# MLP up products of three of four chunks as seven products of half blocks, on one Trainium2 core

## What is computed

```python
def sqrelu_mlp(h, w_up, w_down):          # h 512x1024, w_up 1024x4096, w_down 4096x1024
    return jnp.square(jax.nn.relu(h @ w_up)) @ w_down
...
        x = x + rmsnorm(m, g_mix_post[i])
        h = rmsnorm(x, g_ffn_pre[i])
        x = x + rmsnorm(sqrelu_mlp(h, mlp_w_up[i], mlp_w_down[i]), g_ffn_post[i])
```

## Time and profile before

| | us |
|---|---|
| median of 3 runs | 1156.62 (1155.4 to 1156.87) |
| profiled execution | 1155.48 |
| its span, first to last instruction | 1153.3 |
| TensorE busy | 1130.8 (98%) |
| VectorE, ScalarE, GpSimd busy | 902.0, 676.9, 213.4 |

### The profile page before, as it was taken

The page is one execution under the profiler, slowest core; times in us unless marked ns, Lnnn a source line. Parts: engine busy times, 40 slices in busy tenths (PEclk is TensorE's granted clock), DMA queues, the critical chain, the costliest instruction groups (busy, mean ns, idle before and its releaser), DMA issues. The chain is left out here.

```text
span 1153.3 us, 16246 instructions
## 1 busy us (share of the span) xinstructions
PE 1130.8 (98%) x5598; PEld 951.6 (83%) x5598; DVE 902.0 (78%) x1386; ACT 676.9 (59%) x1168; POOL 213.4 (19%) x205
## 2 busy tenths in 40 slices
PE   8999999999999999999999999999999999999997
PEld 7788888888888888888977888878888888888886
DVE  5899965778479578589789888875797588586698
ACT  6778877565344353445787777765565453443453
POOL 5688860300000000002421111100300000000003
PEclk9999999999999999999999999999999999999999
DMA  5322123321522514313223332232424315215301
GB/s 166 100 70 73 37 76 107 113 74 39 180 73 72 171 50 129 128 37 73 56 55 90 80 86 64 82 83 73 146 74 135 120 37 173 84 37 183 109 19 73
DMA packets 104939, 104.66 MB, mean 91 GB/s; under 512 B 4861, under 2 KB 86781, under 8 KB 104874
## 3 DMA queue, kind: packets, MB, share of 16 engines
q1 hardware_dynamic: 103532, 101.29, 27.4%
q0 software_dynamic: 1264, 2.36, 1.2%
q10 hardware_dynamic: 78, 0.16, 0.1%
HBM read 99.34 MB, written 2.10 MB: 88 GB/s over the span
## 5 line engine op out<-in xcount | busy, mean ns | idle before, releaser
L695 PE MATMUL psum<-hhi,whi 128*128 128x512 f32 x760 | 300.1, 395 | 0.8 <-DVE wlo L1825 0.5
L697 PE MATMUL psum<-hhi,wlo 128*128 128x512 f32 x760 | 296.3, 390 | 0.0
L696 PE MATMUL psum<-hlo,whi 128*128 128x512 f32 x760 | 296.1, 390 | 0.0
L1270 ACT ACTIVATE whi<-mraw 128x1024 fp32r<-128x1024 f32 x176 | 185.5, 1055 | 143.1 <-PE psum L992 113.5
L1836 DVE TENSOR_TENSOR wlo<-mraw,whi 128x1024 fp32r<-128x1024 f32 x176 | 214.4, 1224 | 42.5 <-ACT whi L1270 42.5
L990 PE MATMUL psum<-whi,aop_hi 128*128 128x512 f32 x448 | 174.9, 390 | 0.0
L992 PE MATMUL psum<-whi,aop_lo 128*128 128x512 f32 x448 | 174.4, 389 | 0.0
L991 PE MATMUL psum<-wlo,aop_hi 128*128 128x512 f32 x448 | 174.3, 389 | 0.0
L697 PEld LDWEIGHTS psum<-hhi,wlo 128*128 128x128 f32 x760 | 142.6, 188 | 30.4
L695 PEld LDWEIGHTS psum<-hhi,whi 128*128 128x128 f32 x760 | 142.7, 188 | 29.5 <-issue 1.8
L696 PEld LDWEIGHTS psum<-hlo,whi 128*128 128x128 f32 x760 | 142.8, 188 | 28.0
(11 more groups left out here) (268 smaller groups left out, 2040.0 us busy)
## 6 DMA issues: line engine op xcount, KB each, us to landing
mraw<-in_mlp_w_up SPq DMA_DIRECT2D x64, 512.0 KB, 5.0
mraw<-in_mlp_w_down SPq DMA_DIRECT2D x64, 512.0 KB, 4.6
wraw<-in_conv_pw_w SPq DMA_DIRECT2D x20, 512.0 KB, 4.4
wraw<-in_attn_w_in SPq DMA_DIRECT2D x16, 512.0 KB, 5.0
wraw<-in_attn_w_in SPq DMA_DIRECT2D x16, 256.0 KB, 3.2
wraw<-in_attn_w_o SPq DMA_DIRECT2D x8, 512.0 KB, 4.1
xin<-in_x SPq DMA_DIRECT2D x4, 512.0 KB, 7.0
wraw<-in_conv_pw_w SPq DMA_DIRECT2D x8, 256.0 KB, 6.7
```

The costliest lines, as they stand in the source:

```text
L695: pe.matmul(o, whi[:, u, kb, :], xhi, start=start, stop=False)
L696: pe.matmul(o, whi[:, u, kb, :], xlo, start=False, stop=False)
L697: return pe.matmul(o, wlo[:, u, kb, :], xhi, start=False, stop=stop)
L1270: a.activation(split_unit(whi, e), raw_unit(c, e_), ACT.Copy).then_inc(s["m_hi"], 1)
```

## The change

- **Up stage of chunks 2 to 4** (`up_product`): by the same scheme of seven products, over halves of the inner dimension and of the tokens, and for each of two groups of hidden columns (h). A chunk's up stage has 14 units, each of 2 x 4 x 3 matmuls of 256 columns, in the order P1, P7, P6, P2, P5, P4, P3. Partial sums are copied by ScalarE (`copy_product`), added by VectorE (`c_add2`), and relu and square are both ScalarE's (`take`). Forms and rests of two row blocks are made by one instruction (`s7_of` and so on). The first chunk's up stage stays with eight blocks.
- **h's forms**: `h_whole` makes h in xT's place during the first chunk's up stage (8 instructions of 512 columns), `h_sum` the sums S5, S7, S2, S4, `form_hi_of` and `form_rest` the two parts of the seven forms (full-size instructions of ScalarE and VectorE). As xT is overwritten, x goes to HBM before (`x_copy`) and comes back at the start of the last down stage.
- **Weight sums**: P5 and P6 by VectorE, P7 and P4 by DMAs with addition from HBM, issued by GpSimd (`block_sums`, 28 of 512 KB per MLP), for the down stages too.
- **Numbering**: 106 units per MLP instead of 88; from unit 7 on, unit e goes to buffer (e + 2) % 4, so units 7 and 8 wait for two units more than the others do. Raw slots rotate in another order, and loads are issued by half slots. The first chunk's up columns are loaded in pairs from its two halves.
- A few entries of the attention's hand-written orders move. Some semaphores are used twice.

The diff, cut:

```diff
-UNITS = 22
-MLP_UNITS = CHUNKS * UNITS
+DOWN_UNITS = 14
+UP_OF = (UP_UNITS, 14, 14, 14)
+BASE = (0, 22, 50, 78)
+DOWN = tuple(b + u for b, u in zip(BASE, UP_OF))
+MLP_UNITS = 106
+SHIFT_AT = 7
+def slot(e):
+    return (e if e < SHIFT_AT else e + 2) % 4
...
+UP_ORDER = (P1, P7, P6, P2, P5, P4, P3)
+UP_BLOCK = {P1: B11, P7: B12, P6: B11, P2: B21, P5: B12, P4: B11, P3: B22}
+UP_AT = {i: n for n, i in enumerate(UP_ORDER)}
...
+                for j, b in enumerate((B11, B21, B12, B22)):
+                    for h in range(2):
+                        down_half(0, b, h, 2 * j + 2)
+                    if j == 1:
+                        sp.wait_ge(s["x_done"], (KB, 3 * KB)[l])
+                        sp.dma_start(x_copy, flat(xT[:, :, :])).then_inc(x_kept, 16)
+                for c in range(1, CHUNKS):
+                    n, u = DOWN[c - 1], BASE[c]
+                    for b, at_ in ((B12, 3), (B11, 9), (B21, 11), (B22, 13)):
+                        for h in range(2):
+                            up_half(c, b, h, n + at_ + h)
+                    for h in range(2):
+                        for b, at_ in ((B11, P2), (B21, P5), (B12, P4), (B22, P3)):
+                            down_half(c, b, h, u + 7 * h + UP_AT[at_] + 1)
+                sp.wait_ge(s["m_unit"], MLP_UNITS * l + DOWN[CHUNKS - 1])
+                sp.dma_start(flat(xT[:, :, :]), x_copy).then_inc(x_kept, 16)
...
-            ("T", 7), ("P", 10), ("P", 11), ("O", 1)]
+            ("P", 10), ("T", 7), ("P", 11), ("O", 1)]
...
-ACT_LAST = [("SPLIT", 2), ("S", 0), ("X", -1), ("S", 1), ("T", 0), ("S", 2), ("S", 3), ("T", 1), ("VSPLIT", 0),
+ACT_LAST = [("SPLIT", 2), ("S", 0), ("S", 1), ("X", -1), ("SPLIT", 3), ("T", 0), ("S", 2), ("S", 3), ("T", 1), ("VSPLIT", 0),
...
+            def add_up(l, c, i, h):
+                r = up_slots(l, c)
+                if i == P7:
+                    pool.wait_ge(*loaded(r[B12], h, 2 * (CHUNKS * l + c) + 1))
+                    pool.wait_ge(v7_sum[h], 16 * (v7_nth(l, c, "up", h) - 1))
+                    g.dma_start(raw_half(r[B12], h, 2 * P), up_block(l, c, B22, h),
+                                accum_op=ALU.add).then_inc(v7_sum[h], 16)
+                else:
+                    pool.wait_ge(s["m_ready"], MLP_UNITS * l + BASE[c] + 7 * h + UP_AT[P6] + 1)
+                    pool.wait_ge(s["t_sum"], t_nth(l, c, "up", 2 * h + 1))
+                    g.dma_start(raw_half(r[B11], h, 2 * P), up_block(l, c, B21, h),
+                                accum_op=ALU.add).then_inc(v4_sum[h], 16)
...
+            def block_sums(l):
+                for c in range(CHUNKS):
+                    for i in (P7, P4):
+                        for h in range(2):
+                            add_down(l, c, i, h)
+                        for h in range(2 if c < CHUNKS - 1 else 0):
+                            add_up(l, c + 1, i, h)
...
+            def up_product(l, c, h, i):
+                e, n = BASE[c] + 7 * h + UP_AT[i], 3 * l + c - 1
+                pe.wait_ge(s["m_ready"], MLP_UNITS * l + e + 1)
+                pe.wait_ge(form_lo, lo_nth + 7 * l + H_NTH[FORM[i]])
+                if i == P1:
+                    pe.wait_ge(s["p_evac"], 5 * (CHUNKS * l + c))
+                    bank = Y_BANK[h]
...
+                for t in range(2):
+                    o = by_tile(bank)[:, t, :]
+                    for k in range(4):
+                        w = slice(k * 2 * P + t * P, k * 2 * P + (t + 1) * P)
+                        first = i in (P1, P7) and t == 0 and k == 0
+                        pe.matmul(o, wh[:, w], xh[:, k, :], start=first, stop=False, skip_group_check=True)
+                        pe.matmul(o, wh[:, w], xl[:, k, :], start=False, stop=False, skip_group_check=True)
+                        mm = pe.matmul(o, wl[:, w], xh[:, k, :], start=False, stop=k == 3, skip_group_check=True)
+                mm.then_inc(s["m_unit"], 1)
...
-                    act.wait_ge(s["m_unit"], MLP_UNITS * l + e - 3)
...
+                    act.wait_ge(s["m_unit"], MLP_UNITS * l + e - (1 if e in (SHIFT_AT, SHIFT_AT + 1) else 3))
...
+            def take(l, c, h, q):
+                g, n = CHUNKS * l + c, 3 * l + c - 1
+                at_ = pair[:, 2 * h:2 * h + 2, C_SLOT[q], :]
+                if q in (C11_, C12_):
+                    i, bank = (P2, X_COPY) if q == C11_ else (P3, Y_BANK[h])
+                    act.wait_ge(s["m_unit"], MLP_UNITS * l + BASE[c] + 7 * h + UP_AT[i] + 1)
+                    from_ = by_tile(bank)
+                else:
+                    act.wait_ge(c_sum2, sum2_nth + 4 * n + 2 * h + (1 if q == C22_ else 2))
+                    from_ = at_
+                nth = 8 * n + 4 * h + q + 1
+                a.activation(at_, from_, ACT.Relu,
+                             scale=-1.0 if q in (C12_, C22_) else 1.0).then_inc(c_taken, 1)
+                act.wait_ge(c_taken, taken_nth + nth)
+                a.activation(at_, at_, ACT.Square).then_inc(s["a_sq"], 1)
...
+                n = DOWN[0]
+                for i, forms in enumerate(((A11, S7), (A12,), (S2,), (S5, A22), (S4,))):
+                    m_hi(l, n + 4 + 2 * i)
+                    m_hi(l, n + 5 + 2 * i)
+                    if i < 4:
+                        keep_product(l, i)
+                    for form in forms:
+                        form_hi_of(l, form)
+                m_hi(l, n + 14)
+                keep_product(l, P7)
+                m_hi(l, n + 15)
+                m_hi(l, n + 16)
...
+                for c in range(1, CHUNKS):
+                    g, n = CHUNKS * l + c, BASE[c]
+                    m_hi(l, n + 3)
+                    m_hi(l, n + 4)
+                    copy_product(l, c, 0, CX)
+                    m_hi(l, n + 5)
+                    copy_product(l, c, 0, CZ)
+                    m_hi(l, n + 6)
+                    copy_product(l, c, 0, CU)
+                    m_hi(l, n + 7)
+                    take(l, c, 0, C11_)
+                    m_hi(l, n + 8)
+                    take(l, c, 0, C22_)
+                    m_hi(l, n + 9)
+                    take(l, c, 0, C21_)
+                    m_hi(l, n + 10)
+                    take(l, c, 0, C12_)
+                    a1_hi_of(g, 0)
...
+                    m_hi(l, n + 16)
+                    take(l, c, 1, C21_)
+                    a1_hi_of(g, 1)
+                    take(l, c, 1, C12_)
+                    m_hi(l, n + 17)
+                    a2_hi_of(g, 1)
+                    m_hi(l, n + 18)
+                    s_hi_of(g, 1)
...
+            def add_up_block(l, c, i, h):
+                r, half = up_slots(l, c), slice(h * D, (h + 1) * D)
+                at_ = MLP_UNITS * l + BASE[c] + 7 * h
+                b11, b12 = mraw[:, r[B11], half], mraw[:, r[B12], half]
+                if i == P6:
+                    dve.wait_ge(s["m_ready"], at_ + UP_AT[P1] + 1)
+                    dve.wait_ge(v7_sum[h], 16 * v7_nth(l, c, "up", h))
+                    d.tensor_tensor(b11, b11, b12, ALU.add).then_inc(s["t_sum"], 1)
+                else:
+                    dve.wait_ge(s["m_ready"], at_ + UP_AT[P7] + 1)
+                    dve.wait_ge(s["t_sum"], t_nth(l, c, "up", 2 * h))
+                    dve.wait_ge(*loaded(r[B22], h, 2 * (CHUNKS * l + c) + 1))
+                    d.tensor_tensor(b12, b11, mraw[:, r[B22], half], ALU.subtract).then_inc(s["t_sum"], 1)
+            def h_whole(l, k):
+                if k == 0:
+                    dve.wait_ge(x_kept, 16 * (kept_nth + 2 * l + 1))
+                d.scalar_tensor_tensor(xT[:, k, :], xT[:, k, :], vcol(V_FFN_PRE + l, k), rinv[:, :], ALU.mult,
+                                       ALU.mult).then_inc(h_made, 1)
+            def h_sum(l, form):
+                first = made_nth + 12 * l + KB
+                o = form_of[form]
+                if form == S5:
+                    dve.wait_ge(h_made, first)
+                    d.tensor_tensor(o, form_of[A22], form_of[S7], ALU.subtract).then_inc(h_made, 1)
+                if form == S7:
+                    dve.wait_ge(h_made, first + 1)
+                    d.tensor_tensor(o, form_of[A11], o, ALU.subtract).then_inc(h_made, 1)
...
+            def form_rest(l, form):
+                o = form_of[form]
+                d.tensor_tensor(form_low[form], o, form_high[form].bitcast(F32), ALU.subtract).then_inc(form_lo, 1)
...
+            def first_up(l):
+                g = CHUNKS * l
                 for i in range(4):
                     relu(g, 2 * i)
-                    if early:
-                        if i:
-                            s_lo(g, i - 1)
+                    if i:
+                        s_lo(g, i - 1)
+                    if i < 3:
                         relu(g, 2 * i + 1)
                         m_lo(l, i + 6)
                         s7(g, i)
                     else:
-                        if c == 0:
-                            s_lo(g, i - 1)
-                        m_lo(l, n + 2 * i + 3)
+                        m_lo(l, 9)
```

(81 more changed lines are left out.)

557 lines of the change are left out of this document (370 added, 187 removed).

## The result

The changed kernel takes 1182.12 us (median of four runs, 1181.17 to 1182.78) against 1156.21 us (1155.4 to 1156.87) for the kernel before on the same chip: ratio 1.0223, 95% interval 1.0211 to 1.0236. The forecast was 1165.5 us with a range of 1149 to 1180. The direction was right; the size was not: +26 us where +9 had been worked out, 2 us above the top of the range.

A forecast was written before the change was run, and what follows sets the result against it. TensorE, busy 1130.8 of 1153.3 us, was taken as the bound: 1155.5 - 19.2 (Part 1) + 22.2 (Part 2) + 6 (Part 3), plus 1.1 from trace to median, gave 1165.5 us; range 1149 to 1180.

The forecast's parts named there:

- Part 1: Up stages of chunks 2 to 4: 336 matmuls of 256 columns at 0.120 us replace 192 of 512, saving 19.2 us.
- Rival E: Up stages: halved matmuls take half of a long one, 0.1134 us, saving 32.5 us, total 1152.3 us; chance 0.03.
- Part 2: First chunk of each MLP: buffer step, `h_whole` and `h_sum` delay VectorE's splits, costing 11.1 us per MLP, 22.2 in all.
- the walk: Step-by-step timing of engine queues; first chunk has `m_lo(12)` 10.1 us late, later chunks have a tight up stage end.
- Part 3: End of the new up stages: TensorE waits 1.0 us, mainly for unit 19's split, six times, 6 us; bounds 0 to 15.
- Rival D: TensorE's 4.0 us standstill in the first down stage drops the clock, adding at most 1 us per MLP; within the forecast's 0.68.
- Part 4: Adding transfers land in 5 to 8 us and cost nothing; ScalarE may wait for P4's weights to about 8.3.
- rival B: Adding transfers landing 10.5 us after trigger hold up P5 through ScalarE's queue, 26 us in all, 1192 us; chance 0.07.
- Rivals A and C: A: nothing lost in first chunks, 1143.4 us, chance 0.12. C: level, parts 1 to 3 at 21, 17, 3, 1155.6 us, chance 0.10.
- The costs of zero: Copy of x, other loads and adding transfers cost nothing; reordered attention lists 0, within 0.5 us either way.

The follow-up runs named there:

- keep_clock: Changed kernel with 30 filler matmuls on TensorE ahead of its first long wait in each first down stage; 1182.18 us, ratio 1.0219.
- block_early: `p1_first` with P5's second block sum moved earlier, between S7 and the split of A11, in later down stages; 1165.30 us, ratio 1.0076.
- shift_late: Changed kernel with the step by two buffers at weight unit 20 instead of unit 7; 1184.72 us, ratio 1.0242.
- later_fixed: `p1_first` with P5's second block sum moved later, behind P1's addition, in the later down stages; 1206.43 us, ratio 1.0426.
- p1_first: Changed kernel with P1's addition ahead of P6's first block sum on VectorE in down stages of chunks 2 to 4; 1172.33 us, ratio 1.0137.
- tuned: `block_early` with the step by two buffers at unit 102 and the first down stage's evacuations of P2, P5, P6 ahead of splits; 1157.55 us, ratio 1.0017.
- gates_later: `tuned` with GpSimd's subtraction for the gates' weights held until VectorE has split the MLP's last unit; 1155.18 us, ratio 0.9992.
- pool_two: Changed kernel with `later_fixed`'s moves, step at unit 100, first-chunk sums and evacuations reordered, `h_whole` on GpSimd; 1204.61 us, ratio 1.0422.

## Why the prediction was right and wrong, step by step

**Part 1** was right: 40.31 us, 19.3 us saved against 19.2. Rival E is out: the matmuls stand 0.120 us apart. The estimated 109 ns of the Trainium skill (TensorE: Matmul & The Clock Gate, section Back-to-back issue gap) does not hold in this stream either.

**Part 2** was right in its mechanism and nearly in its size, 12.2 us per MLP instead of 11.1. `m_lo(12)` came 0.5 us later than walked. Behind it I had 0.95 us for VectorE's splits; in the trace the stage lost 1.6, and the wait in it is one of 1.0 us for P2's evacuation on ScalarE. (TensorE's four waits sum to 8.4 us; most of the rest of the 12.2 is matmuls at the lower clock, which by `keep_clock` only fill time that VectorE needs anyway.) Both of its causes are shown: moving the step away takes 5.9 us (44.36), leaving out `h_whole` another 4.9 (39.42). What the walk did not say, though the earlier trace rows with the earlier trace rows would have borne it, is the simple sum: 14.8 us more of VectorE work make 64.7 us for two stages of 59.9. With it one sees at once that, as long as this work stays in these two stages, no order of it brings the down stage below 42.8 us (64.7 - 21.9), and that the step comes on top; with the step gone, 44.3 were measured.

**Part 3 is the step that failed.** It put 1.0 us on each later down stage, 6 us in all, bounds 0 to 15; measured were 23.5. The walk's times were right: `s_lo_of` done at the up stage's start + 51.2 by the walk, + 51.5 in the trace (364.81 - 313.31). It compared P5's first matmul with `s_lo_of` alone. It wrote "block sum and product" behind it and gave them to unit 19, without asking who else waits for that product. P5 does, through P1's PSUM banks, and it gets them at + 53.9 where it wants them at + 51.2. That is the missed term: the stage is 2.9 us longer than 38.08 instead of 1.0. P1's addition ahead of the block sum takes 1.1 us from the wait at P5 (1.98 to 0.83) and 0.7 from the stage, the earlier block sum of P5 another 1.1. With those two moves the stage is 1.0 us over 38.08 (39.1, `block_early`). That is part 3's figure, but by luck: TensorE then loses 0.4 us at P5 and 0.4 at P6, again to VectorE's additions, and nothing at the split of unit 19, where part 3 had put its loss. Part 3 also laid 37.5 us of VectorE's work into the up stage; in the trace it is busy there for 29.6 us, and the forms of the second half run in the down stage.

On top of that came the clock, 1.6 us in four of the six (42.55 against 40.94 us for the same wait of 2.0, clock 0.96 and 1.00 in the rows above), 6.4 of the 23.5. How many of the six it hits is not fixed: `keep_clock` and `shift_late` have the same waits there and two falls each. **Rival D** had it only in the first down stage, and there it is free, as reckoned (`keep_clock`). In the later stages, where VectorE has slack behind the wait, nothing hides it, and there I had not looked.

**Part 4** was right for the kernel as it is: 6.0 us to land, no wait of TensorE. What the Trainium skill's box on "DVE blocks DMA" (SBUF — State Buffer, section SBUF: two separate sides) warns of does not show here: GpSimd's transfers landed in 6.0 us with VectorE busy for 29.6 of 40.3 us of an up stage, all of it subtractions and sums. (The box speaks of VectorE in a 2-port performance mode; no run shows whether any of these operations is in one.) But **rival B** is one moved block sum away, and its chain was right, and its place in the first half of the stage: P4's weights came 13.1 us into the stage (3.7 + 9.4) in `later_fixed`, 4.8 after the 8.3 of part 4. TensorE waited 4.6 to 5.7 us for the copy, and with the lower clock behind it (0.93 in these stages) they are 7.1 to 8.3 us longer. I had looked for a landing that is slow by itself; issue and landing both slip, when VectorE is late and a plain load goes out first.

**Rivals A and C** fell with the first chunk: `m_lo(12)` was over 10 us late, where A needed under 6.5.

The costs of zero held or did better: the copy of x made no wait of TensorE, and between the MLPs the time is 1.2 us less than before, where part 4 had 0 within 0.5.

Shown by their own runs: the step's price, P1's banks, the amount of work, the free clock in the first stage, the transfer's place and ScalarE's queue, GpSimd beside VectorE. The clock's 1.6 us rest on pairs of stages within one trace, on the same stages in `keep_clock`, and on `p1_first`. Not settled is whether an adding transfer behind a plain load is slower because it queues or because it shares the engines; the runs only show that the order decides.

## What to carry to other kernels

When a change shortens TensorE's work, list for each product who frees its PSUM bank, and find that operation in the other engine's queue: a wait for a bank is as hard as one for an operand, and a walk that follows only operands misses it. Before walking an order, add up the busy time of the second engine over the stretch; where it exceeds TensorE's, order within the stretch cannot help, and only work taken out of it does (here by an adding transfer, 2.1 us for 2.35). And a moved operation takes along all that waits for it: one block sum of 1.1 us, moved by 5 us, cost 34 us by way of a transfer.

## What the hardware did that I had not expected

- GpSimd and VectorE hold each other up where both read two inputs from SBUF: on VectorE 415 becomes 1510 ns beside an operation of 1.3 us, 1.22 becomes 3.38 us beside one of 2.72, and 1.22 again when that is moved away; relu with an input in PSUM stays at 680 ns. In `tuned` VectorE's started second and grew, in the kernel before GpSimd's did (4.43 us; 2.40 in `gates_later`, where the two do not meet).
- The Trainium skill (SBUF — State Buffer, section Who interferes with whom) says that a VectorE instruction with two SBUF inputs contends with a GpSimd instruction that reads SBUF. For GpSimd's `tensor_tensor` the runs agree; beside its `tensor_scalar` VectorE kept its 0.95 us (`pool_two`), so there they do not, and the measurement decides.
- Work moved to GpSimd there saved VectorE nothing: 6 us taken off, the stage 2.7 us longer.
- GpSimd's `tensor_scalar` with 128x512 took 2.4 to 2.7 us, twice its `tensor_tensor` (1.3). VectorE was busy all the while, so what it takes alone is not shown.
- An adding transfer of 512 KB lands in 5.8 to 6.0 us if it goes out ahead of the next plain load, and in 9.4 to 9.5 if that load is 0.4 us ahead of the end of GpSimd's instruction.
- The granted clock fell to 1.2 GHz behind waits of 2.0 us in four stages of six and stayed at 2.4 GHz in two; in `keep_clock`, with the same waits, it fell in two and stayed in four. Behind the waits of 0.8 us in `p1_first` it stayed up in all six.
